# Input norms taken per token and the recurrent head norm on 128 partitions, in a two-block fp32 kernel

## What is computed

```python
mod = jax.nn.silu(c) @ w_ada[l] + b_ada[l]        # 6 x 1024, for x; mod_c the same, for ctx
mixed = _mixer(_modulate(ctx, sh1c, sc1c), _modulate(x, sh1, sc1), rows, w_in[l], conv_w[l], ...)
x = _layernorm(ALPHA * x + g1 * (mixed[:, CTX_LEN:] @ w_out[l]), ln1_g[l], ln1_b[l])

def _modulate(z, shift, scale):
    return _layernorm(z) * (1 + scale) + shift     # mean and variance over 1024

# end of the recurrent group, 8 heads of 64, scanned forwards and backwards:
y = _headnorm(_dir_merge(y), GN_EPS) * gn_w.reshape(H_R, D_HR) + gn_b.reshape(H_R, D_HR)
bonus = jnp.sum(r * kmod * bonus_w, -1, keepdims=True) * v
return (y + bonus).reshape(b, t, W_R) * g
```

## Time and profile before

| | |
|---|---|
| three runs | 2172.15 us median (2164.03 to 2172.21) |
| the profiled execution | 2172.35 us, of which the traced span 2170.5 us |
| TensorE busy | 2002.7 us, 92% of the span |
| VectorE, ScalarE, GpSimd busy | 758.1, 411.6, 40.0 us |
| loads | 509 MB from HBM, 235 GB/s over the span |
| granted TensorE clock, mean | 0.951 of full speed |

### The profile page before, as it was taken

One profiled execution on the slowest core, in us unless ns is written; L12 is line 12 of the kernel. 1 busy time (PEld: TensorE's weight loads), 2 busy tenths in 40 slices (PEclk: granted clock), 3 DMA queues, 4 the chain that ended last, 5 costly groups with the idle time before them and its releaser, 6 DMA issues.

```text
span 2170.5 us, 33812 instructions
## 1 busy us (share of the span) xinstructions
PE 2002.7 (92%) x14839; PEld 1347.4 (62%) x14839; DVE 758.1 (35%) x1602; ACT 411.6 (19%) x866; POOL 40.0 (2%) x34
## 2 busy tenths in 40 slices
PE   6999886897999999999899899999898799999998
PEld 4554665586645445555474688887787677463565
DVE  4594378655411111111233245333672420000002
ACT  2200335221311111111134310003231120000001
POOL 1000111000000000000000000000000000000000
PEclk9999896699999999999999999999997799999999
DMA  9710002405589999999775178763300039999991
GB/s 320 271 39 0 1 1 79 156 3 199 228 345 426 425 429 429 430 431 428 299 269 208 61 279 327 259 243 135 138 2 2 1 140 382 396 410 403 410 382 57
DMA packets 162047, 512.34 MB, mean 236 GB/s; under 512 B 9039, under 2 KB 32382, under 8 KB 149246
## 3 DMA queue, kind: packets, MB, share of 16 engines
q1 hardware_dynamic: 146432, 480.65, 56.2%
q10 hardware_dynamic: 15485, 29.77, 3.7%
HBM read 509.35 MB, written 1.05 MB: 235 GB/s over the span
## 4 chain that ended last, share of the span: by engine, by line
PE 85%; DVE 7%; ACT 4%; DMA 2%; issue 2%; POOL 0%; SPq 0%; ACTq 0%; DVEq 0%; POOLq 0%
PE PS L389 28%; PE PS L2467 10%; PE PS L2491 5%; PE PS L2303 4%; PE PS L2589 3%; PE PS L2382 3%; PE PS L2393 3%; PE PS L2581 2%; PE PS L2657 2%; PE PS L2593 2%; PE PS L3140 1%; PE PS L860 1%; DMA work<-in_moe_w_gate_up_dram 1%; PE PS L2660 1%; PE PS L2567 1%
## 5 line engine op out<-in xcount | busy, mean ns | idle before, releaser
L389 PE MATMUL PS<-hT,work 128*128 128x256 f32 x1440 | 327.5, 388 | 4.5 <-ACT hT L928 4.0
L389 PEld LDWEIGHTS PS<-hT,work 128*128 128x128 f32 x1440 | 277.6, 194 | 50.4 <-issue 10.6
L389 PE MATMUL PS<-work 128*128 128x256 f32 (+1 forms) x752 | 231.7, 468 | 2.4 <-DVE work L2040 1.5
L2467 PE MATMUL PS<-work,sq 128*64 128x512 f32 x1024 | 222.6, 592 | 0.0
L389 PEld LDWEIGHTS PS<-work 128*128 128x128 f32 x752 | 145.4, 194 | 86.2 <-issue 69.6
L2467 PEld LDWEIGHTS PS<-work,sq 128*64 128x64 f32 x1024 | 76.6, 137 | 143.2 <-issue 142.5
L2491 PE MATMUL PS<-work 128*64 128x512 f32 x512 | 113.4, 595 | 10.0 <-issue 8.6
L2581 PE MATMUL PS<-work,sq 128*64 128x512 f32 (+1 forms) x384 | 79.0, 569 | 6.1 <-DMA work<-in_moe_w_gate_up_dram 6.1
L2491 PEld LDWEIGHTS PS<-work 128*64 128x64 f32 x512 | 36.8, 137 | 76.3 <-issue 74.4
L2535 DVE TENSOR_TENSOR work<-work,PS 128x64 f32<-128x64 f32 x128 | 18.2, 213 | 184.3 <-PE PS L2467 184.3
L2303 PE MATMUL PS<-work 128*128 128x256 f32 x352 | 76.3, 379 | 0.0
(11 more groups left out here) (631 smaller groups left out, 2597.4 us busy)
## 6 DMA issues: line engine op xcount, KB each, us to landing
work<-in_ex_gate_dram SPq DMA_DIRECT2D x32, 2048.0 KB, 12.9
work<-in_ex_up_dram SPq DMA_DIRECT2D x32, 2048.0 KB, 15.6
work<-in_ex_down_dram SPq DMA_DIRECT2D x32, 2048.0 KB, 11.2
work<-in_moe_w_gate_up_dram SPq DMA_DIRECT2D x32, 2048.0 KB, 13.6
work<-in_moe_w_down_dram SPq DMA_DIRECT2D x16, 2048.0 KB, 17.0
work<-in_ada_w_dram ACTq DMA_DIRECT2D x14, 2048.0 KB, 11.5
work<-in_moe_w_gate_up_dram SPq DMA_DIRECT2D x16, 1536.0 KB, 14.8
work<-in_ada_w_dram SPq DMA_DIRECT2D x10, 2048.0 KB, 13.6
```

Of the source, the lines that this page charges most:

```text
L389: ins = pe.matmul(outp, lhs, rhs, start=n == 0, stop=n == len(pairs) - 1, **kw)
L2467: ins = pe.matmul(PS[pair[m], 6 + j, :], xs[:, k, pair[m]], unit(U[name] + 3 * m + j, KT, F)[:, k, :], start=k == 0, stop=k == KT - 1)
```

## The change

**Input norms.** `ctx` and `x` land in `sq` and `xc`, and mean and variance are taken while the tokens are still rows: VectorE sums each 128 tokens (`token_sums_dve`), ScalarE squares and sums (`token_squares_act`), VectorE scales (`tokens_scaled_dve`), and only then TensorE turns the result (`normed_turn_pe`, L519), which ScalarE copies into place. `x` is also turned unnormed, for the residual, with ALPHA in the copy. The sums by ones are gone. VectorE alone modulates (`modulated_dve`, L592), both streams of a channel tile together, and the first tile of `w_in_pe` takes the channel tiles as they come. ScalarE issues 18 loads of rows ahead of its squares and 11 behind. `later_sp` comes after the load of `("w_in", 0)`.

**The end of the recurrence.** The two directions of a step go to the two halves of the PSUM partitions and alternate from matmul to matmul, `yr` is 128 partitions by 2 parts by 512, and each norm operation has half as many elements per partition. Part 0 is scaled inside step 7. `w_out` is loaded after the last scores (`rw_sc` at 16), and of its first four tiles the mLSTM half (4 of 8 matmuls) is done before `mixed` is 3.

```diff
+    tok = [t.rearrange("p k n -> p (k n)").rearrange("p (t n) -> p t n", t=2) for t in (sq, xc)]
+    ntok = [hT.rearrange("p k n -> p (k n)").rearrange("p (t n) -> p t n", t=2),
+            work[:, ABOVE + 4096:ABOVE + 6144].rearrange("p (t n) -> p t n", t=2)]
...
                 load(place["w_in", j], ktiles(A["w_in"][0], GATES, 352))
-            if (name, j) == ("w_in", 7):
+            if (name, j) == ("w_in", 0):
                 later_sp()
...
     def w_in_pe():
-        normed(pe, 1)
         arrived(place["w_in", 7])
+        w = unit(place["w_in", 7], KT, 352)
+        o = tile_begin("w_in", 0)
+        for k in range(KT):
+            pe.wait_ge(S["norm_done"], 2 * k + 2)
+            ins = pe.matmul(o, w[:, k, 32:160], hall[:, k, :], start=k == 0, stop=k == KT - 1)
+        ins.then_inc(S["tile_full"], 1)
         pe.wait_ge(S["zeroed"], 5)
-        o = tile_begin("w_in", 0)
+        o = tile_begin("w_in", 1)
         product(o[0:104, :], [(w_gate[:, k, :], hall[:, k, :]) for k in range(KT)]).then_inc(S["tile_full"], 1)
-        w = unit(place["w_in", 7], KT, 352)
-        product(tile_begin("w_in", 1), [(w[:, k, 32:160], hall[:, k, :]) for k in range(KT)]).then_inc(S["tile_full"], 1)
...
+    def token_turn_pe(i, src):
+
+        b = TOKEN_BANKS[i % 2]
+        if i >= 2:
+            pe.wait_ge(S["x_evac"], i - 1)
+        for k in range(KT):
+            ins = pe.transpose(PS[:, b + k // 4, (k % 4) * P:(k % 4 + 1) * P], src[:, k * P:(k + 1) * P], ident)
+        ins.then_inc(S["turned"], 1)
+
...
+    def normed_turn_pe(t):
+
+        pe.wait_ge(S["norm_scaled"], t + 1)
+        token_turn_pe(2 + t, ntok[t // 2][:, t % 2, :])
...
+    def token_sums_dve():
+
+        dve.wait_ge(S["tokens"], 32)
+        for t in range(4):
+            dv.link(dve.tensor_reduce(tsum[:, t:t + 1], tok[t // 2][:, t % 2, :], AX.X, ALU.add))
+            dve.tensor_scalar(nmean[:, t:t + 1], tsum[:, t:t + 1], -1.0 / D, None, ALU.mult).then_inc(S["norm_centred"], 1)
+
+    def token_squares_act():
+
+        for t in range(4):
+            act.wait_ge(S["norm_centred"], t + 1)
+            act.activation(squared[:, t, :], tok[t // 2][:, t % 2, :], ACT.Square, bias=nmean[:, t:t + 1], accum_out=tsq[:, t:t + 1])\
+               .then_inc(S["norm_sq"], 1)
+        act.wait_ge(S["norm_sq"], 4)
+        act.activation(tstd, tsq, ACT.Sqrt, scale=1.0 / D, bias=LN_EPS).then_inc(S["norm_std"], 2)
+
+    def tokens_scaled_dve():
+
+        dve.wait_ge(S["norm_std"], 2)
+        dv.link(dve.reciprocal(tstd, tstd))
+        for t in range(4):
+            dve.tensor_scalar(ntok[t // 2][:, t % 2, :], tok[t // 2][:, t % 2, :], nmean[:, t:t + 1], tstd[:, t:t + 1], ALU.add,
+                              ALU.mult).then_inc(S["norm_scaled"], 1)
+
+    def modulated_dve():
+
+        dve.wait_ge(S["x_evac"], 6)
+        for k in range(KT):
+            for which in (1, 0):
+                x = hall[:, k, (1 - which) * N:(2 - which) * N]
+                dve.tensor_scalar(x, x, mod1[:, 8 + k, which:which + 1], mod1[:, k, which:which + 1], ALU.mult, ALU.add)\
+                   .then_inc(S["norm_done"], 1)
...
+        return buf[:, part, :].rearrange("p (h e) -> p h e", e=C)
...
-                ins = pe.transpose(PS[:, 4 * n * part + p, c * C:(c + 1) * C], buf[0:C, c, p * P:(p + 1) * P], ident[0:C, 0:C])
+            ins = pe.transpose(PS[:, 2 + part, p * P:(p + 1) * P], yr[:, part, p * P:(p + 1) * P], ident)
...
     def rw_y_pe(i):
-
         a = i % 2
-        for d in range(2):
-            c = ORDER[d][i]
-            for h in range(H):
-                o = PS[0:C, h % 2, (4 * d + h // 2) * C:(4 * d + h // 2 + 1) * C]
-                pe.matmul(o, KR[half(h), d, h // 2, c * P + C:(c + 1) * P], St[half(h), a, d, h // 2, :],
-                          start=d == 0 and h < 2, stop=False, skip_group_check=True)
-            for h in range(H):
-                o = PS[0:C, h % 2, (4 * d + h // 2) * C:(4 * d + h // 2 + 1) * C]
-                ins = pe.matmul(o, Msc[:, a, d * H + h, C:P], UV[:, c, h * C:(h + 1) * C], start=False, stop=True,
+        cs = [ORDER[d][i] for d in range(2)]
+
+        def at(d, h):
+            return PS[half(int(cs[d] >= 6)), h % 2, (h // 2) * C:(h // 2 + 1) * C]
+
+        for h in range(H):
+            for d in range(2):
+                pe.matmul(at(d, h), KR[half(h), d, h // 2, cs[d] * P + C:(cs[d] + 1) * P], St[half(h), a, d, h // 2, :],
+                          start=h < 2, stop=False, skip_group_check=True)
+        for h in range(H):
+            for d in range(2):
+                ins = pe.matmul(at(d, h), Msc[:, a, d * H + h, C:P], UV[:, cs[d], h * C:(h + 1) * C], start=False, stop=True,
                                 skip_group_check=True)
         ins.then_inc(S["rw_y"], 1)
...
-            headnorm_var_dve(0, yr, ysq, ystat, GN_EPS)
+            headnorm_var_dve(0)
+            headnorm_scale_dve(0)
...
             dve.wait_ge(S["rw_y"], i - 3)
-            for d in range(2):
-                dst = yr[0:C, cs[d] - 4, :].rearrange("p (q b v) -> p b q v", b=2, v=C)
-                ins = dve.tensor_tensor(dst, dst, PS[0:C, 0:2, 4 * d * C:4 * (d + 1) * C].rearrange("p b (q v) -> p b q v", v=C),
-                                        ALU.add)
-                if d == 0:
-                    dv.link(ins)
-            ins.then_inc(S["rw_yd"], 1)
+            dst = yr[:, int(i in (4, NCH - 1)), :].rearrange("p (q b v) -> p b q v", b=2, v=C)
+            dve.tensor_tensor(dst, dst, PS[:, 0:2, 0:4 * C].rearrange("p b (q v) -> p b q v", v=C), ALU.add)\
+               .then_inc(S["rw_yd"], 1)
...
+    def w_out_pe():
+
+        def part(m, k0, k1):
+            w = unit(U["w_out"] + m // 4, KT, 512)
+            o = PS[:, 4 + (first_tile["w_out"] + m) % 4, 0:N]
+            for k in range(k0, k1):
+                ins = pe.matmul(o, w[:, k, (m % 4) * P:(m % 4 + 1) * P], mixT[:, k, :], start=k == 0, stop=k == KT - 1)
+            if k1 == KT:
+                ins.then_inc(S["tile_full"], 1)
+
+        pe.wait_ge(S["mixed"], 1)
+        arrived(U["w_out"])
+        for m in range(4):
+            if m == 3:
+                headnorm_pe(1)
+            tile_begin("w_out", m)
+            part(m, 0, 4)
+        pe.wait_ge(S["mixed"], 3)
+        for m in range(KT):
+            if m == 4:
+                arrived(U["w_out"] + 1)
+            if m >= 4:
+                tile_begin("w_out", m)
+            part(m, 4 if m < 4 else 0, KT)
+            if m:
+                norm_first_pe(2, m - 1)
+        norm_first_pe(2, KT - 1)
...
-        first_squares_act(0)
+        param_rows_act(True)
+        token_squares_act()
+        residual_turned_act()
         ada_act(0)
-        first_squares_act(1)
-        first_std_act(0)
+        param_rows_act(False)
+        normed_turned_act(0)
+        normed_turned_act(1)
         ada_act(1)
-        first_std_act(1)
+        normed_turned_act(2)
+        normed_turned_act(3)
         ada_act(2)
         ada_act(3)
-        first_done_act()
         w_in_act()
...
+        sp.wait_ge(S["rw_sc"], 2 * NCH)
+        out_sp("w_out", A["w_out"][0])
         sp.wait_ge(S["rw_y"], NCH - 4)
-        out_sp("w_out", A["w_out"][0])
...
         cond_pe()
-        tokens_in_pe()
-        pe.wait_ge(S["cond"], 1)
-        for n in range(2):
-            for k in range(KT):
-                norm_mean_pe(n, k)
+        residual_turn_pe()
         ada_pe(0)
-        first_squares_pe(0)
+        ada_turn_pe(0)
+        normed_turn_pe(0)
+        normed_turn_pe(1)
         ada_pe(1)
-        ada_turn_pe(0)
-        first_squares_pe(1)
+        normed_turn_pe(2)
+        ada_turn_pe(1)
+        normed_turn_pe(3)
+        ada_pe(2)
         params_pe()
-        ada_pe(2)
-        ada_turn_pe(1)
+        ada_turn_pe(2)
         ada_pe(3)
-        ada_turn_pe(2)
         ada_turn_pe(3)
         w_in_pe()
...
             rw_step_pe(i)
-        headnorm_pe(1, 0, yr)
-        headnorm_pe(1, 1, yr)
-        pe.wait_ge(S["mixed"], 3)
-        out_pe("w_out", mixT, 2)
+        headnorm_pe(0)
+        w_out_pe()
         norm_rest_pe(2)
...
-        tokens_in_dve()
-        first_centred_dve(0)
-        first_centred_dve(1)
-        first_scaled_dve(0)
-        first_scaled_dve(1)
+        token_sums_dve()
+        tokens_scaled_dve()
         stage0_dve()
         ada_first_dve()
-        first_done_dve()
+        modulated_dve()
         conv_dve()
...
-        headnorm_mean_dve(1, yr, ystat)
-        headnorm_var_dve(1, yr, ysq, ystat, GN_EPS)
-        for part in range(2):
-            headnorm_scale_dve(1, part, yr, ystat)
-        for part in range(2):
-            rw_out_dve(part)
+        headnorm_mean_dve(1)
+        headnorm_var_dve(1)
+        rw_out_gated_dve(0)
+        headnorm_scale_dve(1)
+        rw_out_added_dve(0)
+        rw_out_gated_dve(1)
+        rw_out_added_dve(1)
```

178 lines of the change are left out of this document (68 added, 110 removed).

## The result

| | before | the change |
|---|---|---|
| first series of runs | 2170.43 us median of 4 (2164.03 to 2172.21) | 2136.89 us median of 4 (2131.96 to 2138.47) |
| ratio to before, 95% interval | | 0.9847 (0.982 to 0.9874) |
| both kernels in a later series | 2170.89 us median of 11 | 2145.80 us median of 6 (2139.43 to 2147.76), ratio 0.987 (0.9851 to 0.989) |
| profiled execution of the first series, its span | 2172.35, 2170.5 us | 2136.35, 2134.5 us |

What follows compares the result with a forecast made beforehand. It took TensorE, busy 92% of the span, as the bound. The head's 13.2 us and the recurrence end's 16.5 made 29.7 off 2172.35, so 2142.6 us, range 2134 to 2157.

Steps and rivals of the forecast that it cites:

- The head: Start through the projection's first two tiles: first matmul at 37.8 us, tiles done at 53.3 instead of 66.5, 13.2 us earlier.
- I charge 1.7 us: Projection's first two tiles: a likely clock fall after TensorE's sparse stretch costs 1.7 us, bounds nothing and 3.0.
- R1: Rival, head: patchy TensorE work at half clock, 3.4 us on the path, 1.3 more at the projection; 2147.5 us, chance 0.23.
- R3: Rival, head: ScalarE's queue is the new bound, projection starts as late as 48, head gain 3; 2152.8 us, chance 0.05.
- (a): Recurrence steps 4 to 7: alternating outputs shorten the 128-row runs, 1.0 us a step, 4.0 saved; 64-row runs stay at 1.08.
- The page's sentence: Output runs: the skill says different tiles load and multiply in parallel; 64-row runs would halve, sum 2.2 us better.
- (b): VectorE behind the last output: one addition, halved norm operations and a shorter path to complete mixed; 4.3 us saved.
- (c): Output projection: TensorE does half of each of the first four tiles right after the last output; 6.9 us saved.
- (d): Output projection's start: no hole, so the clock stays up; 1.7 us saved.
- (e): End of the recurrence: the transposes of part 1 wait behind the third half tile; 0.4 us lost.
- R2: Rival, tail: only VectorE's part gains, w_out late or outputs not side by side, some 8 us lost; 2150.5 us, chance 0.1.
- I carry both gains to the end undiminished: Behind the head and the recurrence's end: nothing swallows the gains, loads start earlier with TensorE, so 29.7 us reaches the end.

Runs made afterwards that it cites:

- y_grouped: The changed kernel with the outputs of each direction in one run, all eight heads of one direction, then of the other; 2150.19 us, ratio 0.9888.
- w_out_late: The changed kernel with the load of w_out issued behind the last output, as before the change; 2148.30 us in one run.
- head_only: The change without its edits from the recurrence on; 2162.39 us, ratio 0.9957 to the kernel before.
- change_again: The changed kernel once more, unedited, in a later series; 2145.80 us median of six.
- small_loads_early: The changed kernel with later_sp back behind the load of w_in 7; 2140.90 us in one run.

## Why the prediction came out right, step by step

**What bounds the kernel**: right. TensorE is the chain at both places and between them, and SyncE waits 217.8 us for it in the expert loop, as in the earlier trace rows.

**The head**, 13.2 forecast: 12.6 in the first profile, and between 9.7 and 12.8 in the other nine, read at the end of the projection. The path (ada 3, its copy, columns, additions, modulations) and the tail of VectorE behind TensorE were as drawn. The step that failed is the charge for the clock: "I charge 1.7 us" for one place behind the empty stretch, with R1 as another case. In fact they are two charges that fall separately. Where full clock came near 21 us, TensorE was ahead of ada 3 and paid only at the first tile (8.73 for 6.87, five profiles); where it came at 26 to 29 us, the projection started 1.4 to 3.1 us later, and the first tile paid as well in three profiles (8.74 to 8.80: y_grouped, w_out_late, head_only) and hardly in two (7.10: change_again, small_loads_early). So R1's half speed on the path came in five of ten profiles, and cost 1.3 to 2.9 us of lead instead of the 4.7 that R1 had for it. The 1.7 charged for the first tile measured 1.9. (The sums by ones that are gone are 32 matmuls, not the 16 of R1.) ScalarE as a bound (R3): no. It waited, and its squares took 1.15 each.

**(a) The output runs**, 4.0 forecast: 6.0 (74.9 to 68.9 from step 0 to the last output), made of 6.7 in steps 4 to 7 less 0.7 lost ahead of them. The 128-row runs gave what was reckoned. The mis-sized term is "those of 64 rows stay at 1.08": in the same weight-load rows they take 0.56, and in the chain 0.62 for 1.22. The page's sentence, which I had set beside the sum at 2.2 us, was the better guide, and y_grouped shows that it is the order over the four tiles that does it.

**(b) VectorE behind the last output**, 4.3: 3.5. The error is in "it is ready about when the output is": the scale of part 0 ends 0.7 us behind the last output, because its root stood behind a table load of 1.28 us, and the last addition waits for it. (The pieces behind the variance, 0.68, 0.9, 1.0 and 1.4, add up to 4.0 and not 4.1; they took 3.9.)

**(c) The half tiles**, 6.9: 6.9. **(d) The clock kept up**, 1.7: 2.1 to 2.2. **(e)**: the turn of part 1 takes 0.44. The load of `w_out` was issued at 490.56 and landed 11.2 us later in the median of two; the first half tile never waited for it.

From the last output to the end of the output projection that makes 12.2 us where (b) to (e) had 12.5; with (a) 18.2 where the sum had 16.5. **R2** (the outputs not side by side, `w_out` late) fell on the rows of L1885, L1889 and L2049.

**"I carry both gains to the end undiminished"**: near right in the mean of the change's two profiles (30.3 us at the end) and wrong in each. One of the prediction's own signs of being wrong, a gain smaller further on than where it arose, came at the head: 12.6 us were 8.7 at step 0. In the first profile the lead goes, from the second tile to the end: 12.6; +1.1 to the mLSTM's queries; -5.4 over the mLSTM's steps; +0.4 to step 0; +6.0 to the last output; +12.2 over the output projection; -1.7 over the experts; +5.9 over the attention; +4.9 to the end; 36.0 in all. In change_again the same legs are 11.3, +1.1, -5.3, -0.3, +5.3, +12.5, -1.6, 0.0 and +1.6, 24.6 in all. Only the first and the two of the recurrence are the change's work, and they repeat: 30.8 and 29.1. The mLSTM's loss is clock, perhaps a cost of the change, which is not shown; the rise of 9 us behind the experts in the first profile is clock as well, and chance as far as the other profiles tell. The unforeseen legs add up to +5.2 us in one profile and to -4.5 in the other. So it is in part luck that the forecast of 29.7 lies within 2 us of the 31 of all runs: its local terms were nearly right in sum, with (a) 2 us too small, and of the rest it said nothing.
